# Rotary halves swapped by transfers in place of a permutation product, in a two-layer decoder trunk

## The chip, the cores and the metric

The kernel runs on one core of one Trainium2 chip. Its metric is the device time of one execution in microseconds (us), the median of the timed runs.

## The reference, cut to what matters

Two layers with a residual stream of 1024 positions x 1024 columns in float32. Each layer normalizes, projects, mixes, projects back and runs an MLP. Both layers have queries and keys that are rotated by position before attention:

```python
def apply_rope(x, cos, sin):
    x1, x2 = jnp.split(x, 2, axis=-1)            # two halves of 32 columns of a head of 64
    return jnp.concatenate([x1 * cos - x2 * sin, x2 * cos + x1 * sin], axis=-1)

# layer 0: lightning indexer (iq, ik, iw) picks 256 keys for each query, then attention over them
aq = apply_rope(rms_norm(aq, a_q_norm_g), cos, sin); ak = apply_rope(rms_norm(ak, a_k_norm_g), cos, sin)
iq = apply_rope(iq, cos, sin); ik = apply_rope(ik, cos, sin)
sc = einsum('bqhd,bsd->bqhs', iq, ik)            # index scores, 8 heads
score = einsum('bqhs,bqh->bqs', relu(sc) * 64**-0.5, iw * 8**-0.5)
# layer 1: sliding-window attention with sinks
dq = apply_rope(rms_norm(dq, d_q_norm_g), cos, sin); dk = apply_rope(rms_norm(dk, d_k_norm_g), cos, sin)
```

## The kernel before

The kernel is written with explicit semaphores: each engine has its own list of instructions and works through it in order. Activations lie transposed, 128 features on the partitions. An input projection is cut into units of 128 columns, and each unit into two halves of 512 positions. TensorE computes a half as 24 matmuls (8 blocks of k, three each, of weights and activations split into a high and a low part; lines 2477 to 2479) into one of four PSUM banks in turn. The halves are counted by p. Layer 0 projects, in this order, four units of index queries iq (first all four first halves, then the four second ones), one of index keys ik, four of attention queries aq, one of attention keys ak, and then values and the parts of a recurrence. So p = 0 to 7 is iq, 8 and 9 ik, 10 to 17 aq, 18 and 19 ak. These twenty are the list ROPE0; layer 1 has ten more, ROPE1: two of dk and eight of dq.

What happens to a half that is rotated:

- ScalarE evicts it from PSUM into `xg[:, r % 2, :]` (line 1153 or 1156; r numbers the rotations), for attention queries and keys also its square into `sq` (line 1159), and then raises `proj_free`. Before it overwrites xg it waits for the rotation two before (`rope_done`).
- TensorE, one half later (`follow`), multiplies xg by the constant `rot`, a 128x128 permutation with signs, into PSUM bank 4 (line 2638). The same function adds up the squares (lines 2649 and 2659). `FOLLOWED` lists which halves follow which in the beginning.
- VectorE (`rotate`, line 1831) multiplies bank 4 by sinT into `t2` (line 1838; its rows in the trace name the tile t), xg by cosT (line 1839), and adds the two into its destination (line 1842 or 1849). It raises `rot_read` after the first.

During p = 12 to 19 TensorE also computes the index scores, ten items a half between the blocks of the projection (`scores`, lines 2876 and 2877), in two PSUM banks. ScalarE applies relu into `rl`, which has two buffers (line 1458), and VectorE weights and adds them into `score` (`add_scores`, lines 1876 and 1880). Score product m waits until relu m-2 is done, and relu n waits until sum n-2 is done. In VectorE's list the sums of half p+1 stand ahead of rotation p.

The tables sinT and cosT are made at the start from `positions` and `invf` (lines 1777 to 1791, 1490, 1491). `invf` holds the inverse frequencies, one for each partition.

SyncE's list (SP) holds nearly all loads. Weights come as 512 KB pieces into two raw buffers (`load_unit`, line 649), each when the piece two before has been split into its high part (ScalarE, line 1436) and low part (GpSimd, line 810). Behind them stand, in layer 1, loads of the output weights and of x, and four copies of QS inside SBUF (line 764).

Of the kernel before, what the change touches and what calls it, by code (L numbers as in the profile page):

```python
# [33 lines left out]
HD = 64  # L34
# [42 lines left out]
def build(nc, a, inv_freq, out):  # L77
    with ExitStack() as ctx:
# [6 lines left out]
        def sem(name):  # L85
            return ctx.enter_context(nc.semaphore(name))
# [27 lines left out]
        def const(name, cols, dt=F32, size=4):  # L114
            t = at(name, co[0], [P, cols], dt)
            co[0] += (cols * size + 31) // 32 * 32
            return t

        xn = const("xn", 1024)
        ident, head_ones, rot = const("ident", 128), const("head_ones", 128), const("rot", 128)  # L120
        lmask = at("lmask", co[0], [P, 7, P], I8)
        cbias = const("cbias", 256)
        cT = const("cT", N_ROWS)
# [202 lines left out]
        for n in range(U_ALL):  # L326
# [3 lines left out]
            if not in_halves(n):  # L330
# [2 lines left out]

        raw_landed = [sem(f"raw_landed{i}") for i in range(4)]
        root_begun = sem("root_begun")
        up_first_hi, up_first_lo = sem("up_first_hi"), sem("up_first_lo")
        sums_ready, shared_zero, u_positive = sem("sums_ready"), sem("shared_zero"), sem("u_positive")
        w_hi_ready, w_ready = sem("w_hi_ready"), sem("w_ready")
# [1 line left out]
        own_act, own_dve, own_pool = sem("own_act"), sem("own_dve"), sem("own_pool")  # L340
        (const_landed, cs_saved, cs_landed, consts_built, tables_arg, tables_ready, ct_turned, ct_ready, small_arg,
         small_exp, n_sd, n_xn, n_turned, n_hi, n_lo, proj_done, proj_free, down_done, x_added, u_hi_ready, u_squared, u_ready,
         rot_done, rot_read, rope_done, sq_used, sdq_ready, sdk_ready, rq_ready, iw_turned, iw_ready, ik_copied,
         v_turned, v_ready, sc_done, sc_read, sc_added, thr_ready, level_ready, level_counted, signs_back, gain_landed, vb_saved, lf_ready, b_ready, keys_chosen,
         masks_ready, gw_zero, gw_landed, conv_done, gate_done, gate_read, a_ready, frac_ready, root_ready, oc_ready,
         oc_hi, oc_lo, out_saved) = (sem(n) for n in (
             "const_landed cs_saved cs_landed consts_built tables_arg tables_ready ct_turned ct_ready small_arg "
             "small_exp n_sd n_xn n_turned n_hi n_lo proj_done proj_free down_done x_added u_hi_ready u_squared u_ready "
             "rot_done rot_read rope_done sq_used sdq_ready sdk_ready rq_ready iw_turned iw_ready ik_copied "
             "v_turned v_ready sc_done sc_read sc_added thr_ready level_ready level_counted signs_back gain_landed vb_saved lf_ready b_ready keys_chosen "  # L350
             "masks_ready gw_zero gw_landed conv_done gate_done gate_read a_ready frac_ready root_ready oc_ready "
             "oc_hi oc_lo out_saved").split())
# [286 lines left out]
        def _(sp):  # L639
# [31 lines left out]
            sp.dma_start(posi[:], a["positions"].to_broadcast((P, S))).then_inc(const_landed, 16)  # L671
            sp.dma_start(invf[:], inv_freq).then_inc(const_landed, 16)
            sp.dma_start(sinkb[:], a["d_sinks"].to_broadcast((P, 8))).then_inc(const_landed, 16)
            for n, (_, _, pieces) in enumerate(MIX0):
                if n >= 2:
                    load_unit(n, pieces)
                if n == 3:

                    sp.wait_ge(tables_ready, 2)
                    sp.dma_start(scr_cs[:, 0, :], cosT[:]).then_inc(cs_saved, 16)  # L680
                    sp.dma_start(scr_cs[:, 1, :], sinT[:]).then_inc(cs_saved, 16)
# [55 lines left out]
            load_out(U_OUT0, a["even_w_out"], range(6, N_OUT))  # L737
            load_mlp(U_MLP0, 0)
            for n, (_, _, pieces) in enumerate(MIX1):
                load_unit(U_MIX1 + n, pieces)  # L740
                if n == 2:
                    for t in range(T):
                        sp.wait_ge(x_added, G_MLP0 + S_SUMS * S_ITERS + 2 * t + 2)
                        sp.dma_start(scr_x[:, t, :], x[:, t, :]).then_inc(x_saved, 16)

                    sp.wait_ge(gw_zero, 1)
                    for i, w in enumerate(("c_rgate_w", "c_igate_w")):
                        blocks = a[w][0].rearrange("(n two) c d -> two c n d", two=2)
                        for par in range(2):
                            rows_ = slice(par * HD, par * HD + HD)  # L750
                            sp.dma_start(gw[rows_, 4 * i:4 * i + 4, rows_], blocks[par]).then_inc(gw_landed, 16)
            load_out(U_OUT1, a["odd_w_out"], range(2))
            sp.wait_ge(x_saved, 16 * T)
            sp.wait_ge(oc_ready, 4)
            for t in OC_TILES:
# [29 lines left out]
        def _(pool):  # L785
# [92 lines left out]
                for n in range(n0 + S_UNITS * S_ITERS, n0 + MLP_UNITS):  # L878
                    split_unit(n)

            for t, v in ((ident, 0.0), (head_ones, 0.0), (rot, 0.0), (epsc, EPS), (onec, 1.0)):
                own.link(g.memset(t[:], v))
            own.link(g.affine_select(out=ident[:], in_=ident[:], compare_op=ALU.not_equal, fill=1.0, base=0,
                                     pattern=[[-1, P]], channel_multiplier=1))
            for h in range(2):
                own.link(g.memset(head_ones[h * HD:(h + 1) * HD, h * HD:(h + 1) * HD], 1.0))
            for c, k0, v in ((0, 32, -1.0), (32, 0, 1.0), (64, 96, -1.0), (96, 64, 1.0)):
                own.link(g.affine_select(out=rot[:, c:c + 32], in_=rot[:, c:c + 32], compare_op=ALU.not_equal,
                                         fill=v, base=-k0, pattern=[[-1, 32]], channel_multiplier=1))
            window_and_causal_masks().then_inc(consts_built, 1)  # L890
            def spread_scales(layer, q):

# [820 lines left out]
        def _(dve):  # L1713
# [60 lines left out]

            dve.wait_ge(const_landed, 16 * N_CONST_DMAS)
            link = own.link
            link(v.tensor_copy(pf[:], posi[:]))
            link(v.tensor_scalar(ang[:], pf[:], invf[:, 0:1], None, ALU.mult))

# [51 lines left out]
            def rotate(layer, kind, j, hf):  # L1831
                r = rope_index(layer, kind, j, hf)
                tk = slice(hf * HT, (hf + 1) * HT)
                b = r % 2
                dve.wait_ge(rot_done, r + 1)
                if kind == "ik":
                    dve.wait_ge(iw_turned, hf + 1)
                v.tensor_tensor(t2[:, b, :], ps[:, 4, :], sinT[:, tk], ALU.mult).then_inc(rot_read, 1)
                link(v.tensor_tensor(xg[:, b, :], xg[:, b, :], cosT[:, tk], ALU.mult))
                dve.wait_ge(rot_read, r + 1)  # L1840
                if kind in ("ak", "dk"):
                    link(v.tensor_tensor(t2[:, b, :], xg[:, b, :], t2[:, b, :], ALU.add))
                    dve.wait_ge(sdk_ready, 2 * layer + hf + 1)
                    link(v.reciprocal(key_rms[layer][:], key_rms[layer][:]))
                    dst = (kT if layer == 0 else dkT)[:, tk]
                    v.tensor_tensor(dst, t2[:, b, :], key_rms[layer][:], ALU.mult).then_inc(rope_done, 1)
                else:
                    dst = {"iq": iqT, "aq": qT, "dq": dqT}[kind][:, j, tk] if kind != "ik" else ikT[:, tk]
                    v.tensor_tensor(dst, xg[:, b, :], t2[:, b, :], ALU.add).then_inc(rope_done, 1)
# [44 lines left out]
            for p, (kind, j, hf) in enumerate(ROPE0):  # L1894

                if p == 4:
                    small_arguments()
                if 6 <= p < 9:
                    small_results(p - 6)
                if p == SC_FIRST - 3:  # L1900
                    index_query_low(2)
                    index_query_low(3)
                if p + 2 == SC_FIRST:
                    index_key_low(0)
                if p + 1 == SC_FIRST:
                    dve.wait_ge(iw_ready, 2)
                for n in sc_items(p + 1):
                    add_scores(n)
                rotate(0, kind, j, hf)
                if p + 1 == SC_FIRST:  # L1910
                    index_key_low(1)
            query_scale(0)
# [545 lines left out]
        def _(pe):  # L2458
# [168 lines left out]

            def rope_products(layer, kind, j, hf, p):
                r = rope_index(layer, kind, j, hf)
                pe.wait_ge(proj_free, p + 1)  # L2630
                if r >= 1:
                    pe.wait_ge(rot_read, r)
                if r == 0:

                    pe.wait_ge(n_lo, 14)
                if r == len(ROPE0):
                    pe.wait_ge(gate_read, 8)
                t_.matmul(ps[:, 4, :], rot[:], xg[:, r % 2, :], start=True, stop=True).then_inc(rot_done, 1)
                if kind in ("aq", "dq"):

                    q = sq_index(layer, kind, j, hf)
# [41 lines left out]
            def turn_spread_scales(layer, q):  # L2683
                pe.wait_ge(rq_spread, T * layer + q + 1)
                if layer == 0:
                    bank = (4, 5)[q % 2]
                    if q >= 2:
                        pe.wait_ge(att["q_scaled"], q - 1)
                    elif q:

                        pe.wait_ge(v_ready, 2)
                    else:
                        pe.wait_ge(rot_read, len(ROPE0))
                else:
                    bank = (7, 4)[q % 2]
                    if q >= 2:
                        pe.wait_ge(att["q_scaled"], T + q - 1)
                    else:
                        pe.wait_ge(rot_read, len(ROPE0) + len(ROPE1))
                for j in range(4):  # L2700
                    ins = t_.transpose(ps[:, bank, j * P:(j + 1) * P], rqb[layer][:, q % 2, j * P:(j + 1) * P], ident[:])
                ins.then_inc(att["q_turned"], 1)
# [373 lines left out]
```

## Time and profile before

| | us |
|---|---|
| median of 3 runs | 2543.17 |
| lowest and highest run | 2540.28, 2543.9 |
| span of the profiled execution | 2541.8 |
| TensorE busy in it | 2454.6 |
| VectorE busy | 1611.6 |
| ScalarE busy | 1060.7 |
| GpSimd busy | 1292.5 |

The profile comes from one execution. The execution's own time is not listed apart from its span. Matmuls overlap in it: a row says how long one lasts from its start to its end, and the distance between the starts of two says what one costs TensorE. Bracketed at the end of a row of the order of time is how long the engine had been idle before it, and what ended that. The mean granted clock of TensorE is 0.984 of full speed.

### The profile page before, as it was taken

What the parts mean: (1) busy time and instruction counts of PE and PEld (TensorE: products, weight loads), DVE (VectorE), ACT (ScalarE), POOL (GpSimd) and SP (SyncE); (2) the same over time, 40 slices, a digit from 0 to 9 for tenths busy, and PEclk for the clock granted to TensorE, in tenths of its full rate; (3) what the DMA queues carried; (4) which work ended last, traced back from release to release, by engine and by line L of the source; (5) the groups of instructions that cost most, each with busy time, mean ns of one, the idle gap of its engine ahead of it and who ended that gap; (6) DMA issues with size and microseconds to landing.
All of it is one profiled execution on the core that took longest, in us unless ns stands there. A gap on an engine that the chain in (4) does not pass through costs nothing. (4 is left out here: it accounts for less than half of the span.)

```text
span 2541.8 us, 31069 instructions
## 1 busy us (share of the span) xinstructions
PE 2454.6 (97%) x11111; PEld 1952.5 (77%) x11133; DVE 1611.6 (63%) x2336; ACT 1060.7 (42%) x1821; POOL 1292.5 (51%) x681
## 2 busy tenths in 40 slices
PE   8999998998999999999999999979999999999999
PEld 6778875557888888888888877757687888888887
DVE  6778878988875654465448656675546544564483
ACT  4456887666645332223222356254452322332210
POOL 3212325888863664576449221164337645665490
PEclk9999998999999999999999999979999999999999
DMA  4200121004001210221112231030112111211121
GB/s 150 50 26 26 42 83 51 1 17 133 10 25 51 66 34 33 66 66 50 33 50 59 74 96 42 25 108 13 50 34 67 43 40 50 66 58 33 41 66 67
DMA packets 159545, 133.00 MB, mean 52 GB/s; under 512 B 22537, under 2 KB 134226, under 8 KB 159442
## 3 DMA queue, kind: packets, MB, share of 16 engines
q1 hardware_dynamic: 152978, 125.10, 16.3%
q10 hardware_dynamic: 6464, 6.56, 0.9%
q8 instruction: 61, 1.00, 0.2%
q14 instruction: 42, 0.34, 0.0%
HBM read 116.17 MB, written 13.63 MB: 51 GB/s over the span
## 5 line engine op out<-in xcount | busy, mean ns | idle before, releaser
L2477 PE MATMUL ps<-h_hi,w_hi 128*128 128x512 f32 x1672 | 661.5, 396 | 0.0
L2479 PE MATMUL ps<-h_hi,w_lo 128*128 128x512 f32 x1672 | 651.9, 390 | 0.0
L2478 PE MATMUL ps<-h_lo,w_hi 128*128 128x512 f32 x1672 | 651.4, 390 | 0.0
L810 POOL TENSOR_TENSOR w_lo<-w_raw,w_hi 128x1024 fp32r<-128x1024 f32 x69 | 184.2, 2669 | 361.3 <-ACT w_hi L1436 357.7
L2479 PEld LDWEIGHTS ps<-h_hi,w_lo 128*128 128x128 f32 x1672 | 314.1, 188 | 66.4
L2477 PEld LDWEIGHTS ps<-h_hi,w_hi 128*128 128x128 f32 x1672 | 314.3, 188 | 66.1 <-issue 3.8
L2478 PEld LDWEIGHTS ps<-h_lo,w_hi 128*128 128x128 f32 x1672 | 314.4, 188 | 65.9 <-issue 3.4
L2361 DVE TENSOR_TENSOR x_res<-ps,x_res 128x1024 f32<-128x1024 f32 x224 | 268.7, 1220 | 115.6 <-PE ps L2479 115.6
L828 POOL TENSOR_TENSOR w_lo<-w_raw,w_hi 128x1024 fp32r<-128x1024 f32 x112 | 267.3, 2402 | 127.3 <-ACT w_hi L1298 90.0
L2342 DVE TENSOR_TENSOR u_all<-ps,u_all 128x512 f32<-128x512 f32 x112 | 77.0, 690 | 380.3 <-ACT u_all L1309 380.3
L2477 PE MATMUL ps<-w_hi,uo_hi 128*128 128x512 f32 x784 | 307.9, 393 | 4.9 <-DVE shared L2361 3.5
L2479 PE MATMUL ps<-w_hi,uo_lo 128*128 128x512 f32 x784 | 305.7, 390 | 0.0
L2478 PE MATMUL ps<-w_lo,uo_hi 128*128 128x512 f32 x784 | 305.5, 390 | 0.0
L1309 ACT ACTIVATE u_all<-ps 128x512 f32<-128x512 f32 x112 | 66.7, 599 | 334.0 <-PE ps L2479 333.1
L828 POOL TENSOR_TENSOR w_lo<-w_sum,w_hi 128x1024 fp32r<-128x1024 f32 x42 | 114.0, 2728 | 147.3 <-ACT w_hi L1298 147.3
L2477 PEld LDWEIGHTS ps<-w_hi,uo_hi 128*128 128x128 f32 x784 | 147.1, 188 | 50.5 <-DVE shared L2361 7.7
L1298 ACT ACTIVATE w_hi<-w_raw 128x1024 fp32r<-128x1024 f32 x107 | 111.3, 1052 | 148.8 <-PE ps L2479 148.8
L2479 PEld LDWEIGHTS ps<-w_hi,uo_lo 128*128 128x128 f32 x784 | 147.2, 188 | 31.7
L2478 PEld LDWEIGHTS ps<-w_lo,uo_hi 128*128 128x128 f32 x784 | 147.3, 188 | 27.4
L1301 ACT ACTIVATE uo_hi<-u_all 128x1024 fp32r<-128x1024 f32 x56 | 59.5, 1063 | 161.9 <-PE ps L2479 151.2
L824 POOL TENSOR_TENSOR uo_lo<-u_all,uo_hi 128x1024 fp32r<-128x1024 f32 x42 | 114.9, 2736 | 0.0
L973 POOL TENSOR_TENSOR PL<-PF,h_hi 128x512 fp32r<-128x512 f32 x72 | 104.3, 1460 | 18.1 <-ACT h_hi L1258 17.9
(385 smaller groups left out, 4490.4 us busy)
## 6 DMA issues: line engine op xcount, KB each, us to landing
w_raw<-in_mlp_w_up SPq DMA_DIRECT2D x64, 512.0 KB, 4.1
w_raw<-in_mlp_w_down SPq DMA_DIRECT2D x64, 512.0 KB, 3.6
w_raw<-in_even_w_in SPq DMA_DIRECT2D x23, 512.0 KB, 3.8
x_res<-in_x SPq DMA_DIRECT2D x16, 512.0 KB, 7.9
w_raw<-in_odd_w_in SPq DMA_DIRECT2D x10, 512.0 KB, 3.9
scr_x<-x_res SPq DMA_DIRECT2D x8, 512.0 KB, 2.6
x_res<-scr_x SPq DMA_DIRECT2D x8, 512.0 KB, 4.4
out<-x_res SPq DMA_DIRECT2D x8, 512.0 KB, 2.6
```

Source lines behind the costliest of these rows:

```text
L810: g.tensor_tensor(w_lo[:, k, :], w_raw[:, n % 2, :], w_hi[:, k, :].bitcast(F32), ALU.subtract).then_inc(w_ready, 1)
L824: g.tensor_tensor(uo_lo[o][:], source, uo_hi[o][:].bitcast(F32), ALU.subtract).then_inc(u_ready, 1)
L828: g.tensor_tensor(w_lo[:, slot, :], source, w_hi[:, slot, :].bitcast(F32), ALU.subtract) \
L973: g.tensor_tensor(PL[n % 3][:], PF[n % 3][:], PH[:, n % 3, :].bitcast(F32), ALU.subtract) \
L1298: s.activation(w_hi[:, slot, :], source, ACT.Copy).then_inc(w_hi_ready, 1)
L1301: s.activation(uo_hi[S_OPERAND[k]][:], source, ACT.Copy).then_inc(u_hi_ready, 1)
L1309: s.activation(u_all[:, j, hf * HT:(hf + 1) * HT], ps[:, (h0 + p + UP_BANK) % 4, :], ACT.Relu).then_inc(u_positive, 1)
L2342: v.tensor_tensor(part, src, part, ALU.mult).then_inc(proj_free, 1)
L2361: ins = v.tensor_tensor(dst, ps[:, bank:bank + 2, :], dst, ALU.add)
L2477: t_.matmul(out_, ah, bh, start=first, stop=False)
L2478: t_.matmul(out_, ah, bl, start=False, stop=False)
L2479: return t_.matmul(out_, al, bh, start=False, stop=last)
```

## The change

The product with `rot` goes. In its place SyncE makes four transfers for each rotated half, inside SBUF, of 32 partitions each: rows 32 to 63 of xg go to rows 0 to 31 of t2, 0 to 31 to 32 to 63, and the same for the upper 64. It waits for `proj_free` of that half first, and the four raise `half_moved` of the buffer by 64. The transfers stand at fixed places among the weight loads. VectorE waits for `half_moved`, and its first multiply reads t2 in SBUF instead of bank 4; the signs are put into sinT by negating invf for rows 0 to 31 and 64 to 95. The constant rot and the five instructions that built it go, and so do the waits of TensorE for `rot_read` and those waits for bank 4 that went with it. For attention queries of layer 0 (aq, p = 10 to 17) rotation p now stands ahead of the sums of half p+1 in VectorE's list; for the other kinds the order stays.

```diff
+            def swap_halves(layer, i):
+                r, p = len(ROPE0) * layer + i, i if layer == 0 else H_MIX1 + 16 + i
+                sp.wait_ge(proj_free, p + 1)
+                for to, of in ((0, 32), (32, 0), (64, 96), (96, 64)):
+                    sp.dma_start(t2[to:to + 32, r % 2, :], xg[of:of + 32, r % 2, :]).then_inc(half_moved[r % 2], 16)
+
+            SWAPPED = {3: (0, 1), 4: (2, 3, 4), 5: (5,), 6: (6,), 7: (7,), 8: (8, 9)}
+            SWAPPED.update({n: (2 * n - 8, 2 * n - 7) for n in range(9, 14)})
             for n, (_, _, pieces) in enumerate(MIX0):
                 if n >= 2:
                     load_unit(n, pieces)
+                for i in SWAPPED.get(n, ()):
+                    swap_halves(0, i)
                 if n == 3:
...
             for n, (_, _, pieces) in enumerate(MIX1):
+                if n == 13:
+                    swap_halves(1, 0)
+                    swap_halves(1, 1)
                 load_unit(U_MIX1 + n, pieces)
...
-            load_out(U_OUT1, a["odd_w_out"], range(2))
+            swap_halves(1, 2)
+            swap_halves(1, 3)
+            load_out(U_OUT1, a["odd_w_out"], range(1))
+            for i in range(4, 10):
+                swap_halves(1, i)
+            load_out(U_OUT1, a["odd_w_out"], range(1, 2))
...
-            for t, v in ((ident, 0.0), (head_ones, 0.0), (rot, 0.0), (epsc, EPS), (onec, 1.0)):
+            for t, v in ((ident, 0.0), (head_ones, 0.0), (epsc, EPS), (onec, 1.0)):
...
-            for c, k0, v in ((0, 32, -1.0), (32, 0, 1.0), (64, 96, -1.0), (96, 64, 1.0)):
-                own.link(g.affine_select(out=rot[:, c:c + 32], in_=rot[:, c:c + 32], compare_op=ALU.not_equal,
-                                         fill=v, base=-k0, pattern=[[-1, 32]], channel_multiplier=1))
...
+            for h in range(2):
+                v.tensor_scalar(invf[h * HD:h * HD + 32, :], invf[h * HD:h * HD + 32, :], -1.0, None, ALU.mult)
...
-                dve.wait_ge(rot_done, r + 1)
+                dve.wait_ge(half_moved[b], 64 * (r // 2 + 1))
                 if kind == "ik":
                     dve.wait_ge(iw_turned, hf + 1)
-                v.tensor_tensor(t2[:, b, :], ps[:, 4, :], sinT[:, tk], ALU.mult).then_inc(rot_read, 1)
+                v.tensor_tensor(t2[:, b, :], t2[:, b, :], sinT[:, tk], ALU.mult).then_inc(rot_read, 1)
...
-                for n in sc_items(p + 1):
-                    add_scores(n)
+                if kind != "aq":
+                    for n in sc_items(p + 1):
+                        add_scores(n)
                 rotate(0, kind, j, hf)
+                if kind == "aq":
+                    for n in sc_items(p + 1):
+                        add_scores(n)
...
             def rope_products(layer, kind, j, hf, p):
                 r = rope_index(layer, kind, j, hf)
+                if kind == "iq":
+                    return
                 pe.wait_ge(proj_free, p + 1)
-                if r >= 1:
-                    pe.wait_ge(rot_read, r)
-                if r == 0:
-
-                    pe.wait_ge(n_lo, 14)
                 if r == len(ROPE0):
                     pe.wait_ge(gate_read, 8)
-                t_.matmul(ps[:, 4, :], rot[:], xg[:, r % 2, :], start=True, stop=True).then_inc(rot_done, 1)
```

## Rows read from the trace of the kernel before

**Rows 1.** Windows: start:end, length, busy PE PEld DVE ACT POOL, clock, DMA share, GB/s.

```profile
210.00:240.00 30.00, 30.00 (x139) 24.36 (x138) 26.62 (x70) 15.53 (x25) 8.84 (x6) 1.00 0.13 36
1620.00:1630.00 10.00, 10.00 (x51) 7.87 (x50) 3.18 (x5) 2.35 (x4) 0.00 (x0) 1.00 0.00 1
```

**Rows 2.** Instructions of line 2638, TensorE: duration min/median/max in ns, first and last start.

```profile
L2638 PE MATMUL ps<-xg,rot x60: 590/591/667, 40.7 to 1646.4; 128*128 128x512 f32 x60
```

**Rows 3.** Order of time, TensorE, 52 to 54 us: start, length, instruction, [idle before].

```profile
52.09 0.39 PE L2478 MATMUL ps<-h_lo,w_hi 128*128 128x512 f32 x1
52.32 0.39 PE L2479 MATMUL ps<-h_hi,w_lo 128*128 128x512 f32 x1
...
53.64 0.40 PE L2478 MATMUL ps<-h_lo,w_hi 128*128 128x512 f32 x1
```

**Rows 4.** Order of time, start-up: ScalarE's eviction of half 4, TensorE's products.

```profile
62.05 0.60 ACT L1153 ACTIVATE xg<-ps 128x512 f32<-128x512 f32 x1 [5.75 <-DVE iqT L1849]
...
67.13 1.10 PE L2638 MATMUL ps<-xg,rot 128*128 128x512 f32 x2 [0.88 <-DVE t L1838]
...
76.62 0.39 PE L2478 MATMUL ps<-h_lo,w_hi 128*128 128x512 f32 x1
```

**Rows 5.** Order of time, TensorE, 100 to 191 us: ends of halves, gated score products.

```profile
101.77 1.02 PE L2638 MATMUL ps<-xg,rot 128*128 128x512 f32 x2
...
107.96 0.44 PE L2876 MATMUL ps<-ikH,iqS 128*128 128x384 f32 x1 [0.78 <-ACT rl L1458]
...
177.57 1.02 PE L2638 MATMUL ps<-xg,rot 128*128 128x512 f32 x2
...
184.05 0.47 PE L2876 MATMUL ps<-ikH,iqS 128*128 128x512 f32 x1 [1.07 <-ACT rl L1458]
190.29 1.02 PE L2638 MATMUL ps<-xg,rot 128*128 128x512 f32 x2
```

**Rows 6.** Order of time, one half behind E(16): TensorE, ScalarE, VectorE.

```profile
165.31 1.02 PE L2638 MATMUL ps<-xg,rot 128*128 128x512 f32 x2
167.37 0.59 ACT L1159 ACTIVATE sq<-ps 128x512 f32<-128x512 f32 x1
168.26 0.68 DVE L1838 TENSOR_TENSOR t<-ps,sinT 128x512 f32<-128x512 f32 x1
170.18 5.02 DVE L1880 SCALAR_TENSOR_TENSOR score<-rl,iw,score 128x512 f32<-128x512 f32 x6
171.67 0.50 PE L2876 MATMUL ps<-ikH,iqS 128*128 128x512 f32 x1 [0.57 <-ACT rl L1458]
```

**Rows 7.** DMA issues by line: QS on SP, on ScalarE's queue, a weight load.

```profile
L764 SPq DMA_DIRECT2D QS<-QS x4: 529/604/613, 1663.4 to 1665.3; - x4
...
DMA to landing us min/median/max: 4.0/4.3/5.0
...
DMA to landing us min/median/max: 2.2/2.4/5.1
...
L649 SPq DMA_DIRECT2D w_raw<-in_even_w_in x31: 367/368/1571, 3.1 to 348.8; - x31
```

**Rows 8.** The longest gate and its clock; a shorter gate and its clock.

```profile
135.12 0.33 PE L2876 MATMUL ps<-ikH,iqS 128*128 128x128 f32 x1 [1.74 <-ACT rl L1458]
...
135.95:139.30 3.35, 3.35 (x11) 2.79 (x10) 1.79 (x5) 0.83 (x3) 0.00 (x0) 0.50 0.10 28
...
159.90 0.39 PE L2876 MATMUL ps<-ikH,iqS 128*128 128x256 f32 x1 [1.41 <-ACT rl L1458]
...
160.00:170.00 10.00, 10.00 (x50) 8.23 (x51) 7.44 (x14) 6.51 (x13) 0.00 (x0) 1.00 0.18 50
```

**Rows 9.** VectorE's two multiplies by line: duration min/median/max in ns, first and last start.

```profile
L1838 DVE TENSOR_TENSOR t<-ps,sinT x30: 680/691/694, 49.8 to 1648.9; 128x512 f32<-128x512 f32 x30
L1839 DVE TENSOR_TENSOR xg<-xg,cosT x30: 677/681/2575, 50.4 to 1649.5; 128x512 f32<-128x512 f32 x30
```

**Rows 10.** Order of time, SP's queue, layer 1.

```profile
1611.29 52.09 SPq L774 DMA_DIRECT2D x_res<-scr_x  x2
```

More of the change, by code:

```diff
@@ L119, in build @@
         xn = const("xn", 1024)
-        ident, head_ones, rot = const("ident", 128), const("head_ones", 128), const("rot", 128)
+        ident, head_ones = const("ident", 128), const("head_ones", 128)
         lmask = at("lmask", co[0], [P, 7, P], I8)
@@ L335, in build @@
         root_begun = sem("root_begun")
+        half_moved = [sem("half_moved0"), sem("half_moved1")]
         up_first_hi, up_first_lo = sem("up_first_hi"), sem("up_first_lo")
@@ L342, in build @@
          small_exp, n_sd, n_xn, n_turned, n_hi, n_lo, proj_done, proj_free, down_done, x_added, u_hi_ready, u_squared, u_ready,
-         rot_done, rot_read, rope_done, sq_used, sdq_ready, sdk_ready, rq_ready, iw_turned, iw_ready, ik_copied,
+         rot_read, rope_done, sq_used, sdq_ready, sdk_ready, rq_ready, iw_turned, iw_ready, ik_copied,
          v_turned, v_ready, sc_done, sc_read, sc_added, thr_ready, level_ready, level_counted, signs_back, gain_landed, vb_saved, lf_ready, b_ready, keys_chosen,
@@ L348, in build @@
              "small_exp n_sd n_xn n_turned n_hi n_lo proj_done proj_free down_done x_added u_hi_ready u_squared u_ready "
-             "rot_done rot_read rope_done sq_used sdq_ready sdk_ready rq_ready iw_turned iw_ready ik_copied "
+             "rot_read rope_done sq_used sdq_ready sdk_ready rq_ready iw_turned iw_ready ik_copied "
              "v_turned v_ready sc_done sc_read sc_added thr_ready level_ready level_counted signs_back gain_landed vb_saved lf_ready b_ready keys_chosen "
@@ L2691, in turn_spread_scales @@
                         pe.wait_ge(v_ready, 2)
-                    else:
-                        pe.wait_ge(rot_read, len(ROPE0))
                 else:
@@ L2697, in turn_spread_scales @@
                         pe.wait_ge(att["q_scaled"], T + q - 1)
-                    else:
-                        pe.wait_ge(rot_read, len(ROPE0) + len(ROPE1))
                 for j in range(4):
```

## The prediction

> **What bounds the kernel now.** I read the page's totals first, then TensorE in windows, then its waits, then the order of time around the places that the diff touches. By the totals TensorE is busy for 2454.6 of 2541.8 us, so the first question for each product removed is whether TensorE ran through at that place. In 210 to 240 us and in 1620 to 1630 us it did, with no idle time at full clock [rows 1]. In 100 to 205 us it did not: in seven halves in a row a score product waits for ScalarE's rl, which waits for VectorE (the first at 107.96 us, the last at 184.05 us) [rows 5]. These are the halves in which VectorE adds scores between two rotations, so there the order on VectorE sets the pace, and the diff changes that order.
>
> **The products removed.** The permutation product shows as 60 rows, two passes each, so 30 products (20 in layer 0, 10 in layer 1) [rows 2]. Its cost on TensorE is not its 591 ns a row but the gap that it leaves: one projection matmul starts 0.23 us behind the other; with a product between, 52.32 to 53.64 us is 1.32 us where two steps of 0.23 would do. That is 0.86 us each [rows 3]; 30 would be 25.8 us.
> I part them by place. E(p) is the time at which TensorE ends the projection of half p (the start of the product behind it).
> - Ahead of E(11) = 101.77 us lie ten products, 8.6 us. Twice a second product waited 0.88 us for VectorE to read bank 4, once at 67.13 us [rows 4]; 1.8 us go with it. Sum -10.4 us. The swap must not take TensorE's place as the thing waited for. The nearest cover: half 4 is evicted at 62.05 us after waiting for a rotation, and TensorE needs that bank free only at the half that begins at about 76.6 us [rows 4]; 14 us of cover, less the 6 us by which the work before it gets shorter, against transfers that can lie behind a 512 KB load.
> - Seven products (behind E(11) to E(17)) lie ahead of a wait that VectorE ends. They give nothing by themselves.
> - Three more (behind E(18), E(19) and the next half) lie where no score waits: -2.6 us.
> - Ten in layer 1, with TensorE busy throughout: -8.6 us.
> Gains: 10.4 + 2.6 + 8.6 = 21.6 us. The five GpSimd instructions on rot, and two negations of a 128x1 column in the tables' chain, lie beside the loads of x and are taken at nothing (a few tenths of a us if that cover is gone). The other waits of TensorE on rot_read that go had been met already and give nothing.
>
> **The rotation moved ahead of the sums.** For p = 11 to 17 VectorE now does rotate(p) and then the ten sums of half p+1; before it was rotate(p-1), whose product had been ready for long. VectorE works in order, so while it waits for the swap, the sums of half p+1 queue behind it; rl has two buffers, so relu 2 needs sum 0, and the fifth score product needs relu 2. That is the gate seen now. I take its time from E(p):
> - Before: 107.96 - 101.77 = 6.2 us for p = 11 and 184.05 - 177.57 = 6.5 us for p = 17 [rows 5]; the seven are 6.2, 7.0, 7.5, 6.7, 6.4, 6.4 and 6.5, mean 6.65 us.
> - After: ScalarE ends xg and sq 1.4, 3.2, 2.2, 1.4, 1.6, 2.7 and 1.4 us behind E(p), mean 1.95 (p = 16: 167.37 + 0.59 - 165.31) [rows 6]; then the four transfers, L; then the rotation, 168.26 to 170.18 us = 1.92 us; then from the first sum to the released score product, 170.18 to 171.67 us = 1.49 us [rows 6]. Gate at 5.36 + L.
> L is shown by no row. SP issues them one after another; the nearest kind is the copy of QS inside SBUF, 0.60 us each on SP and 2.2 us from issue to landing at best, 4.3 us where SP's four stood behind a 512 KB load [rows 7]. Three issues ahead of the last and its landing: 3 x 0.62 + 2.2 = 4.1 us, which I take, since no load is issued ahead of these swaps (loads 11, 12 and 13 come behind an odd swap, and wait for nothing else by then). Low end: issues of 0.37 us, as for w_raw [rows 7]: 3.3 us. High end: 1.9 + 4.3 = 6.2 us.
> The gate moves from 6.65 to 9.46 us, so each of the seven halves takes 2.81 us more, 19.7 us in all (14.1 to 34.4 by L's ends). From the gate to E(p+1) TensorE has its own work left, 190.29 - 184.05 = 6.2 us [rows 5], and VectorE's sums (six in 5.02 us, 0.84 each [rows 6]) keep up with it, so nothing is caught up.
> The Trainium skill's page "DMA: Bandwidth & Descriptors", section "Rules for kernel authors", speaks against this order: issue a DMA early, compute, and wait on its semaphore late. The same page, under where a DMA's fixed cost goes, fits about 2.0 us plus bytes over 436 GB/s, an estimate of 2.15 us for 64 KB; the QS copies' 2.2 us [rows 7] agree, and the sum would be the same within 0.4 us.
>
> **The clock.** TensorE, not gated, would reach the fifth score product 4.6 us behind E(p) (107.96 less the idle 0.78, less 101.77, less the product's 0.86 [rows 5]; a little later with wider score products); at 9.5 us it has been idle for some 4.7 us. The longest such idle time now is 1.74 us, at 135.12 us, and behind it the granted clock was 0.50 (1.2 of 2.4 GHz) from about 135.95 to 139.3 us, 3.4 us at half rate, 1.7 us lost [rows 8]. The shorter gates show no such fall: behind the 1.41 us at 159.90 us the clock stays at 1.00 [rows 8]. So I expect a fall at each of the seven; some of the slow time will lie in the idle time, so 1.5 us each, 10.5 us, less the 1.7 us paid already: +8.8 us (bounds -1.7 and +10.2).
>
> **What else queues behind the new waits.** SP now waits for evictions in order. In layer 0 loads 11 to 13 follow an odd swap and are rounded two halves later; load 13 of layer 1 follows the second swap of dk and is used nine halves later. Behind the last swaps of layer 1 stand the load of output unit 1 and that of x tile 4; the loads of x now stop at 1611 us and go on at 1663 us only [rows 10], so a start at about 1640 us has 20 us of cover. Taken at nothing; if the cover of a load were gone, its 4 us.
>
> **The multiply moved to SBUF.** The first multiply read PSUM and stayed within 680 to 694 ns, the second reads two SBUF tiles and went up to 2575 ns beside GpSimd [rows 9]. The change gives the first the second's form. GpSimd splits a weight just behind every other eviction; the rotation now comes some 4 us later, when that has ended. I take nothing, with 0 to 4 us for the range (two of 1.9). The Trainium skill, page "SBUF — State Buffer", on the shared port pair, says that a VectorE instruction with two SBUF inputs and a GpSimd one exclude each other for a whole instruction; the row agrees.
>
> **Sum.** -21.6 + 19.7 + 8.8 = +6.9 us. The profiled span is 2541.8 us, 1.4 us under the median of three runs, 2543.17; I keep that distance, and 2548.7 + 1.4 = 2550.1 us.
>
> **Rivals.**
> - *Faster: the swap is quick and the clock holds.* One mechanism, the length of VectorE's wait in the score halves. With the clock's 8.8 us the change breaks even at L = 3.1 us; if the clock stays full, at 4.6 us. With L = 4.1 us and no fall: -21.6 + 19.7 - 1.7 = -3.6, 2539.6 us. With 3.3 us and no fall: -9.2, 2534.0 us. For it: idle times of up to 1.4 us left the clock alone. Against: 4.7 us is over twice the 1.74 us that did not. With 3.3 us and the falls it is +1.3, 2544.5 us.
> - *A longer landing.* L = 6.2 us, from packets of other transfers or four small transfers that hinder each other: -21.6 + 34.4 + 8.8 = +21.6, 2564.8 us. For it: SP's own row of four is 4.3 us per transfer. Against: a load stood ahead of those.
> - *The change does what it seems made for*: the wait is covered, as if rl were deep enough, and all products and both bank waits go: -25.8 - 1.8 = -27.6, 2515.6 us. Against: the gates now already follow VectorE's position.
> - *The start.* Swaps behind 512 KB loads hold evictions of halves 2 to 9 so long that TensorE waits: two loads of 4 us give +5 on the forecast, 2555 us.
>
> **How the numbers follow.** Chances: forecast 0.40 (its own range 2544 to 2557); clock holds at L = 4.1, 0.17; short L with falls 0.13 and without 0.07; long landing 0.12; all covered 0.04; start 0.07. Slower or faster by 0.2%, about what a measurement of this kernel can tell from no change, is over 2548.3 or under 2538.1 us. Slower: 0.26 of the forecast, long landing, start: 0.45. Faster: the two without falls and short L, all covered, and a third of the clock case: 0.20. Same: 0.35. The range of 8 in 10 reaches from short L without falls to long landing: 2533 to 2565 us.
>
> **What would show it.** Right: VectorE's first multiply in 90 to 200 us waits 3.5 to 5 us for a transfer, seven times; the score product's wait for rl grows from about 1 to 4 us; the clock row falls in most of those halves; E(18) - E(11) grows from 88.5 us to about 117 us; layer 1 from its first rotary half to the attention is 8.6 us shorter. Wrong: VectorE's waits at 2 us or less (L), clock at 1.00 throughout, or TensorE waiting for evictions ahead of E(11).

## The result, and the profile after

| | before | after |
|---|---|---|
| median, us | 2543.5 | 2560.2 |
| lowest and highest run | 2540.28, 2546.41 | 2555.3, 2563.83 |
| ratio of after to before, 95% interval | | 1.0063 [1.0046, 1.0081] |
| span of the profiled execution | 2541.8 | 2553.6 |
| E(11), the projection of half 11 ended | 101.77 | 93.91 |
| E(18) - E(11), the seven score halves | 88.5 | 118.2 |
| last product with gw (layer 1, just ahead of its rotations) | 1578.6 | 1593.8 |
| last product over squares, layer 1 | 1647.6 | 1654.4 |

The change makes the kernel slower, by 0.6%. The span grew by 11.8 us, the median by 16.7 us: the profiled execution is the fastest of the four of after. The same kernel timed again gave 2556.9 us and 1.0060 [1.0047, 1.0073] (below); one of its six executions took 6150.8 us and is not in that interval, which uses undisturbed executions alone.

The totals, from the page of the kernel after:

```profile
span 2553.6 us, 31058 instructions
PE 2440.7 (96%) x11073; PEld 1947.9 (76%) x11073; DVE 1602.6 (63%) x2338; ACT 1059.9 (42%) x1821; POOL 1291.4 (51%) x676
```

TensorE is busy for 13.9 us less than before and the span is 11.8 us longer. So the question is where it waits. As in the prediction, the gate of a half is the score product that has to wait for rl. Line numbers in rows are those of the kernel that was traced, so the same instruction has another number in each version. Waits of the kernel after from 90 to 215 us (us in total, times, longest), and its windows there (columns as in [rows 1]):

```profile
PE ps L2891 <- ACT rl L1475: 29.5, 10, 4.9
DVE t L1857 <- DMA t<-xg: 25.7, 7, 4.9
```

```profile
104.00:110.00 6.00, 5.98 (x29) 5.17 (x29) 4.45 (x9) 3.49 (x7) 0.00 (x0) 1.00 0.00 0
120.40:126.00 5.60, 5.60 (x18) 4.51 (x19) 3.77 (x7) 2.86 (x5) 0.00 (x0) 0.72 0.00 0
138.00:144.00 6.00, 5.89 (x18) 5.03 (x19) 2.62 (x6) 1.53 (x6) 0.00 (x0) 0.50 0.00 0
154.00:160.00 6.00, 5.93 (x19) 4.69 (x20) 4.88 (x8) 3.59 (x8) 0.00 (x0) 0.72 0.00 0
170.60:176.00 5.40, 5.32 (x19) 4.56 (x20) 2.56 (x6) 1.69 (x6) 0.00 (x0) 0.61 0.00 0
188.00:194.00 6.00, 6.00 (x19) 4.89 (x20) 3.47 (x6) 2.55 (x5) 0.00 (x0) 0.68 0.00 0
204.00:210.00 6.00, 5.76 (x18) 4.62 (x19) 3.71 (x7) 2.38 (x5) 0.00 (x0) 0.72 0.01 3
```

The score product's wait for rl was 7.1 us in eight waits before and is 29.5 us now; VectorE's wait for the swap is new. The windows begin at the seven gates: behind six of them the granted clock (the first number behind the brackets) is 0.50 to 0.72, where two score halves of before showed 0.50 and 1.00 [rows 8]. The first, behind an idle time of 2.36 us, stays at 1.00.

The ends of the projections and the gates, TensorE in order of time, kernel after, that answer to [rows 5]:

```profile
93.91 0.95 PE L2668 MATMUL ps<-head_ones,sq 128*128 128x2 f32 x8
...
104.02 0.44 PE L2891 MATMUL ps<-ikH,iqS 128*128 128x384 f32 x1 [2.36 <-ACT rl L1475]
...
109.90 0.95 PE L2668 MATMUL ps<-head_ones,sq 128*128 128x2 f32 x8
...
120.40 0.80 PE L2891 MATMUL ps<-ikH,iqS 128*128 128x512 f32 x1 [4.90 <-ACT rl L1475]
...
195.65 0.95 PE L2668 MATMUL ps<-head_ones,sq 128*128 128x2 f32 x8
...
204.24 0.47 PE L2891 MATMUL ps<-ikH,iqS 128*128 128x512 f32 x1 [4.03 <-ACT rl L1475]
...
212.07 0.95 PE L2668 MATMUL ps<-head_ones,sq 128*128 128x2 f32 x8
```

The product over the squares now stands first behind a projection, so its start is E(p). The gates stand 10.1, 10.5, 9.5, 8.3, 8.8, 10.0 and 8.6 us behind their E(p), mean 9.4 us (6.65 before; 9.46 predicted).

One such half, behind E(16) = 177.97 us, the rows of the relay in order of time (the half of [rows 6], after):

```profile
180.03 0.59 ACT L1176 ACTIVATE sq<-ps 128x512 f32<-128x512 f32 x1
...
180.64 2.41 SPq L680 DMA_DIRECT2D t<-xg  x4
...
184.51 0.69 DVE L1857 TENSOR_TENSOR t<-t,sinT 128x512 f32<-128x512 f32 x1 [3.51 <-DMA t<-xg]
...
186.44 4.17 DVE L1899 SCALAR_TENSOR_TENSOR score<-rl,iw,score 128x512 f32<-128x512 f32 x5
187.28 0.60 ACT L1475 ACTIVATE rl<-ps 128x512 f32<-128x512 f32 x1 [5.60 <-DVE score L1899]
...
187.93 0.79 PE L2891 MATMUL ps<-ikH,iqS 128*128 128x512 f32 x1 [4.90 <-ACT rl L1475]
...
188.53 0.63 PE L2892 MATMUL ps<-ikL,iqS 128*128 128x512 f32 x1
```

Read it as a relay. The square ends at 180.62, four transfers are issued in 2.41 us, and VectorE begins its multiply at 184.51: L = 3.9 us. From there to the gate are 3.42 us (1.92 + 1.49 predicted). Over the seven halves the three parts have these means: evictions end 2.1 us behind E(p) (1.95 predicted), L 4.0 us (4.1), from the multiply to the gate 3.2 us (3.41). In the first of the seven, VectorE did not wait for the swap: it was still at the rotation before. The five sums stand behind the rotation, relu waited 5.60 us for one of them, and the score product waited 4.90 us for relu. The next product lasts 0.63 us in place of 0.39: the clock has fallen.

### The profile page after: what moved, and what is told of

The parts are those of the page before. It is cut to its first block, busy times and chain, and to the rows that moved or that the text cites. A ratio compares the mean times of both kernels' runs of the same rounds, so it can differ in the third digit from the quotient of the medians.

```text
span 2553.6 us, 31058 instructions
## 1 busy us (share of the span) xinstructions
PE 2440.7 (96%) x11073; PEld 1947.9 (76%) x11073; DVE 1602.6 (63%) x2338; ACT 1059.9 (42%) x1821; POOL 1291.4 (51%) x676
## 4 chain that ended last, share of the span: by engine, by line
PE 73%; DVE 10%; ACT 6%; issue 4%; POOL 3%; DMA 1%; SPq 1%; ACTq 0%; DVEq 0%; POOLq 0%
PE ps L2500 21%; PE ps L2502 21%; PE ps L2501 21%; ACT signs L1430 3%; PE ps L2755 1%; POOL cl L1029 1%; PE ps L2493 1%; DMA t<-xg 1%; DVE ub L2387 1%; PE ps L2763 1%; SPq L680 1%; PE ps L2742 1%; PE ps L2783 1%; DVE shared L2384 1%; PE ps L2786 1%
```

## Experiments

The intervals are those of the ratio to the kernel before, timed on the same chip in the same rounds. "After" is the changed kernel.

**The old order with the swaps.**

```diff
-                if kind != "aq":
-                    for n in sc_items(p + 1):
-                        add_scores(n)
+                for n in sc_items(p + 1):
+                    add_scores(n)
                 rotate(0, kind, j, hf)
-                if kind == "aq":
-                    for n in sc_items(p + 1):
-                        add_scores(n)
```

> The changed kernel with VectorE's old order for the attention queries: the sums of half p+1 ahead of rotation p. The swaps by SyncE stay. My theory (VectorE waits for the swap ahead of the sums, and the score products wait for VectorE): no wait of VectorE for a swap is left between 100 and 210 us, the score products' wait falls from 29.6 us to under 7 us, E(18) - E(11) falls from 118.2 us to about 84 us (12.65 us a half less 0.7), the clock stays at full there, and the time is 2513 to 2525 us, some 40 us under the changed kernel and 18 to 30 us under the kernel before. Rival (the transfers themselves cost: SyncE, queues or SBUF): E(18) - E(11) stays over 100 us and the time stays within 5 us of the kernel before or above it.

2529.1 us, 0.9951 [0.9938, 0.9964]: faster than both kernels, by 12 us and by some 28 us. It lies above the expected 2513 to 2525: the 0.7 us a half that was expected from the products taken out did not come. Two of its waits from 90 to 215 us, and its window:

```profile
PE ps L2887 <- ACT rl L1475: 9.9, 11, 2.0
...
DVE t L1857 <- DMA t<-xg: 0.7, 1, 0.7
```

```profile
100.00:210.00 110.00, 100.08 (x465) 80.14 (x464) 91.70 (x134) 61.54 (x114) 11.55 (x6) 0.98 0.19 48
```

With the sums ahead of the rotation the swap has a whole half of time, VectorE waits 0.7 us for it instead of 25.7, and E(18) - E(11) is 182.39 - 93.05 = 89.3 us. That is within 1 us of the 88.5 us of before: the order alone costs the seven halves 29 us, and the seven products taken out of them give nothing there. The span of this profile is 17.8 us shorter than before, by the start (E(11) 8.7 us earlier) and layer 1 (8.4 us); it is the fastest of six executions, and by the medians the gain is 12.5 us.

**Products kept for aq and ak, swaps for the rest.** The version above, with ten of its thirty swaps, those of aq and ak, as products again; iq, ik and layer 1 stay swapped.

```diff
+        def swapped(r):
+            return r < 10 or r >= 20
...
+                if not swapped(r):
+                    t_.matmul(ps[:, 4, :], rot[:], xg[:, r % 2, :], start=True, stop=True).then_inc(rot_done, 1)
```

> Swaps in layer 1 and for iq and ik of layer 0; aq and ak keep their products and the old order of VectorE. Against the variant with all swapped and the sums first (2529 us): if the products behind E(11) to E(17) are worth nothing because VectorE paces those halves, only two products ahead of E(11) and the last three count, up to 4 us, so 2528 to 2534 us. Rival (each product costs 0.86 us there too): 10 us more, 2538 us or above.

2529.9 us, 0.9951 [0.9938, 0.9964]: not to be told from the version with all thirty swaps. E(18) - E(11) is 183.50 - 96.58 = 86.9 us with the products in it, 89.3 us without. So a product in the score halves costs nothing that a run can show. The expectation counted two kept products ahead of E(11); there is none, the first stands at E(11) itself.

The differences that are left are mostly falls of the clock. The third score half has the same work and the same idle time of 1.74 us here and in before: there the clock is at 0.66 from 135 to 140 us and the half takes 14.0 us, here it is at 1.00 from 129.9 to 134.8 us and the half takes 12.5 us. That is the 1.6 us between 88.5 and 86.9. With the swaps, the first and the fifth half are 1.9 and 1.6 us longer than here, with a clock of 0.78 (94 to 99 us) and 0.69 (150.5 to 156 us) in them.

**Swaps in layer 1 alone.** The kernel before, with its ten last products replaced.

```diff
+        def swapped(r):
+            return r >= 20
```

> The kernel before, with the swaps by SyncE in layer 1 alone; layer 0 keeps its products, in the old order. (The signs sit in sinT for both layers, and rot is a permutation without signs.) My theory: ten products of 0.86 us go where TensorE never idles, so the time is 8.6 us under the kernel before, 2532 to 2536 us, and nothing else moves by over 1 us up to the layer. Rival (SyncE's waits and transfers cost something in layer 1): less than 5 us under it.

2534.5 us, 0.9962 [0.9951, 0.9974], so 9 us under before where 8.6 were forecast. From the last product with gw to the last one over squares its trace is 8.4 us shorter than before, as that of after is. TensorE runs through there, and a product costs its whole gap.

**The clock by itself.** After, with sixteen products whose results nobody reads put into the idle time ahead of the gate. VectorE's wait stays; only TensorE is not idle in it.

```diff
+                        if m == items[4] and p < 19:
+                            for _ in range(16):
+                                t_.matmul(ps[:, 4, :], h_hi[:, 0, 0:P], h_hi[:, 0, 0:HT], start=True, stop=True)
```

> The changed kernel with 16 idle-time matmuls (128x512, into the free PSUM bank 4, read by nobody) on TensorE just ahead of the fifth score product of halves 12 to 18, where it stands idle for 3.8 to 4.9 us. They take 3.7 us at full clock. If the clock falls behind each idle time cost what I said (10.5 us in all), it stays at 1.00 from 100 to 210 us and the time falls by 6 to 11 us against the changed kernel, to about 2550 us. If the clock's fall costs nothing (VectorE's sums set the pace in the slow time as well), the time stays within 3 us of the changed kernel's 2560 us although the clock row stays full. If the matmuls do not fit into the idle time, it is slower by up to 5 us.

2547.9 us, 1.0024 [1.0015, 1.0033], against 1.0060 and 1.0063 without: some 0.37%, 9 us faster, for added work. Two of its waits from 90 to 215 us and two windows behind gates:

```profile
DVE t L1857 <- DMA t<-xg: 28.8, 8, 5.8
...
PE ps L2894 <- ACT rl L1475: 7.0, 11, 2.2
```

```profile
120.00:126.00 6.00, 3.77 (x17) 2.81 (x16) 5.54 (x8) 2.40 (x4) 0.00 (x0) 1.00 0.00 0
137.00:143.00 6.00, 5.70 (x30) 4.52 (x29) 5.05 (x9) 2.12 (x6) 0.00 (x0) 1.00 0.22 65
```

VectorE waits no less (28.8 us, 25.7 in after), the clock is at 1.00 where it was 0.72 and 0.50, and E(18) - E(11) is 205.24 - 94.90 = 110.3 us instead of 118.2. The two parts of the loss come apart: 110.3 - 88.5 = 21.8 us are the later gates, 7.9 us the clock. The 7.9 us are the least that the clock takes, since the sixteen products, 3.7 us, are longer than the first half's idle time and hold its gate back by 1.5 us. The rows of after alone part the same 29.7 us into 19.1 us ahead of the gates (seven times 9.38 - 6.65) and 10.5 us behind them.

**Fewer and more transfers.** The swap of after in two transfers of 64 partitions, and in eight of 32 partitions and half a row. The two exchange the heads in place of the halves of a head, so that kernel computes other values with the same bytes moved; the eight move what after moves. The edit of the two:

```diff
-                for to, of in ((0, 32), (32, 0), (64, 96), (96, 64)):
-                    sp.dma_start(t2[to:to + 32, r % 2, :], xg[of:of + 32, r % 2, :]).then_inc(half_moved[r % 2], 16)
+                for to, of in ((0, 64), (64, 0)):
+                    sp.dma_start(t2[to:to + 64, r % 2, :], xg[of:of + 64, r % 2, :]).then_inc(half_moved[r % 2], 16)
```

> The changed kernel with two transfers of 64 partitions for each rotated half in place of four of 32 (same bytes; it swaps the two heads in place of the halves of a head, so the rotation's values are others). L, from the eviction's end to VectorE's first multiply, falls by two issues of 0.6 us, from about 4.0 to 2.8 us. If the wait of VectorE is passed on one to one, the seven gates come 1.2 us earlier each and E(18) - E(11) falls by 8.4 us from 118.2 us, with less idle time for the clock perhaps by up to 5 us more; the time is 2547 to 2552 us. Rival (landing, not issue, makes up L): below 3 us of change.

> The changed kernel with eight transfers of 32 partitions x 256 columns for each rotated half in place of four of 512 columns (same bytes, same result). Four more issues ahead of the last landing: L grows by 2.4 us, the seven gates come 2.4 us later each, E(18) - E(11) grows by about 17 us from 118.2 us, and the time is 2575 to 2582 us; the clock's loss stays the same. The start may lose 1 to 3 us more. Rival (a loss fixed per half, as from the clock alone): within 4 us of the changed kernel.

Two transfers: 2550.8 us, 1.0034 [1.0021, 1.0048]. Eight: 2587.7 us, 1.0181 [1.0166, 1.0196], 6 us over the upper end of what was expected. The mean gate moves from 9.4 us behind E(p) to 8.5 us and to 11.9 us: two issues fewer take off 0.9 us (two of 0.6, less a landing that is 0.3 us longer), four more add 2.6 us. E(18) - E(11) is 113.6 us (8.4 us under 118.2 were expected) and 138.8 us. The issues of the two kernels (KB each, median us from issue to landing), and of the one with eight the waits from 90 to 215 us:

```profile
t<-xg SPq DMA_DIRECT2D x60, 128.0 KB, 2.3
```

```profile
t<-xg SPq DMA_DIRECT2D x240, 32.0 KB, 1.9
```

```profile
DVE t L1859 <- DMA t<-xg: 41.6, 9, 7.3
...
PE ps L2893 <- ACT rl L1477: 32.4, 8, 7.3
...
PE ps L2685 <- ACT xg L1172: 9.4, 1, 9.4
```

A transfer lands in 1.9 us at 32 KB, 2.0 at 64 and 2.3 at 128, so what counts most is how many are issued one behind the other. Eight also hit the start: TensorE waited 9.4 us once for an eviction, and E(11) was 104.1 us, 10 us later than in after. That is the rival on the start, in sight once the swap is slow enough; with the halves' 20.6 us over after it makes up the 30.7 us between this version and the repeat of after.

**After again.** No edit.

> The changed kernel once more, unedited, to place its time on the same chip as the variants and to see how far single executions scatter: 2555 to 2565 us.

2556.9 us, 1.0060 [1.0047, 1.0073]. The ratio repeats within its interval, and so do the seven halves: E(18) - E(11) is 215.50 - 96.16 = 119.3 us. The start does not: E(11) = 96.16 us, 2.3 us later than in after, with two waits of TensorE for evictions (4.0 us; 3.3 in after) and a clock of 0.87 from 80 to 93 us (1.00 in after).

So one trace does not say what the start gives. All versions whose start has the same swaps at the same places show E(11) at 93.05 (old order), 93.91 (after), 94.90 (filler products), 96.16 and 96.58 us (products kept), 5.2 to 8.7 us ahead of before. With products at the start two traces agree: 101.77 us in before and in the version with layer 1 alone.

**Loads ahead of swaps at the start.** The start gave 7.9 us and not 10.4 us, in after and nearly so in the old order. Here each load from unit 5 on stands ahead of the swaps that it stood behind, in the old order of sums (the edit of that order is left out).

```diff
-            SWAPPED = {3: (0, 1), 4: (2, 3, 4), 5: (5,), 6: (6,), 7: (7,), 8: (8, 9)}
-            SWAPPED.update({n: (2 * n - 8, 2 * n - 7) for n in range(9, 14)})
+            SWAPPED = {3: (0, 1), 5: (2, 3, 4), 6: (5,), 7: (6,), 8: (7,)}
+            SWAPPED.update({n: (2 * n - 10, 2 * n - 9) for n in range(9, 15)})
```

> The variant with all swapped and the sums first, with each weight load of layer 0 from unit 5 on put ahead of the swaps that it stood behind. Between 58 and 90 us ScalarE waits 10.3 us for weight loads that SyncE issued only after a swap. If that wait holds the evictions and makes up the 2.5 us that I missed ahead of E(11), then ScalarE's waits for w_raw go, E(11) comes 2 to 3 us earlier and the time is 2525 to 2528 us. Rival (the swaps now land later behind the loads, and hold the evictions as long): 2529 us or more.

2532.5 us, 0.9959 [0.9946, 0.9972]: no gain over the old order's 0.9951 [0.9938, 0.9964], so the rival holds; a loss is not shown. Waits of the kernel from 34 to 100 us:

```profile
ACT xg L1170 <- DVE iqT L1868: 21.9, 7, 8.3
DVE t L1857 <- DMA t<-xg: 8.9, 4, 6.9
...
PE ps L2679 <- ACT xg L1170: 4.8, 1, 4.8
```

ScalarE's wait for w_raw (10.5 us in the old order with swaps first) is gone, and in its place it waits 21.9 us for rotations (11.1 before the edit), since VectorE waited up to 6.9 us for a swap. E(11) is 97.98 us, behind all five traces above.

**The swaps of iq and ik issued by ScalarE.** Both queues of the start apart: loads on SyncE, swaps behind their own evictions on ScalarE. The old order of sums again.

```diff
-            SWAPPED = {3: (0, 1), 4: (2, 3, 4), 5: (5,), 6: (6,), 7: (7,), 8: (8, 9)}
+            SWAPPED = {}
...
                     s.activation(xg[:, r % 2, :], src, ACT.Copy).then_inc(proj_free, 1)
+                    act.wait_ge(proj_free, p + 1)
+                    for to, of in ((0, 32), (32, 0), (64, 96), (96, 64)):
+                        act.dma_start(t2[to:to + 32, r % 2, :], xg[of:of + 32, r % 2, :]).then_inc(half_moved[r % 2], 16)
```

> The kernel with the old order of sums and rotations (sums of half p+1 ahead of rotation p for aq too), and the ten swaps of iq and ik issued by ScalarE right behind its own eviction instead of by SyncE among the loads; the ten others of layer 0 and layer 1's ten stay on SyncE. Theory (the start's shortfall comes from loads and swaps in one in-order queue): ScalarE's waits for w_raw (10.5 us with the swaps on SyncE) nearly go, without the wait of VectorE for a swap growing to 6.9 us as with the loads put first; the half before the first attention-query sums ends near 91.5 us instead of 93.05, so 1 to 2 us under the version with SyncE's swaps: 2526 to 2529 us. Rival (ScalarE's own time is short here: four issues of some 0.6 us for a half on the engine that evicts and splits weights): TensorE waits for evictions, the half ends at 95 us or later, 2531 us or more.

2531.3 us, 0.9963 [0.9951, 0.9975], E(11) = 98.45 us: the rival again, and again no loss beyond the intervals. In order of time, and the waits from 34 to 100 us:

```profile
52.80 2.68 ACTq L1173 DMA_DIRECT2D t<-xg  x4
...
61.04 0.69 DVE L1860 TENSOR_TENSOR t<-t,sinT 128x512 f32<-128x512 f32 x1 [7.03 <-DMA t<-xg]
```

```profile
DVE t L1860 <- DMA t<-xg: 12.0, 5, 7.0
...
PE ps L2682 <- ACT xg L1170: 3.6, 2, 2.1
```

The swap was issued from 52.80 us and its multiply began at 61.04, though no load stood ahead of it in ScalarE's queue. The issues cost ScalarE 2.4 to 3.5 us a swap as well. So the place in the queue is not all of it. The windows of this kernel, then of after:

```profile
50.00:60.00 10.00, 10.00 (x46) 8.29 (x45) 3.88 (x6) 1.22 (x3) 0.00 (x0) 1.00 0.97 254
```

```profile
50.00:60.00 10.00, 10.00 (x46) 8.29 (x45) 5.36 (x10) 1.20 (x2) 0.00 (x0) 1.00 0.71 212
```

The DMA share (the number ahead of the last) is 0.97 here, 0.71 in after. From the end of the eviction to the multiply this swap takes 52.78 to 61.04 = 8.3 us here and 5.8 us in after, against 3.9 us in the score half above (3.9 to 4.6 in the seven), where the share of 10 us is at most 0.32. In the same 10 us the old order had 0.60 and 6.4 us, the loads ahead 0.91 and 8.1 us. The two highest shares go with the two longest swaps. That loads and swaps share the DMA engines fits; which packet waited for which was not measured.

## Why the prediction was right, point by point

- **Sign and size.** 2550.1 us was forecast, with 2533 to 2565 around it; 2560.2 us came out (2556.9 in the repeat), above or at the end of the forecast's own narrower range, 2544 to 2557. The span grew by 11.8 us where the sum had 6.9; the other 4.9 us between the medians lie in the profiled execution being a fast one. Part of the closeness is luck: two stretches that the sum did not have, of -5.5 and +5.0 us, cancel (below). The 0.20 for faster and 0.35 for same are 0.17 and 0.38 by the parts given for them.
- **The gate.** The largest term, and right in its parts: mean gate 9.4 us behind E(p) (9.46), L = 4.0 us (4.1), 3.2 us from the multiply to the gate (3.41). The gates lie 19.1 us later in all (19.7); with the clock held, the halves took 21.8 us more. VectorE waited 3.4 to 4.9 us for a transfer in six halves, not seven.
- **The clock.** 8.8 us forecast, 7.9 us or somewhat more by the version with filler products. The step that judged each gate by the length of its own idle time does not hold: behind 1.74 us of idle the clock fell in before [rows 8] and stayed at 1.00 in the version with products kept, behind 2.00 and 2.04 us in the old order it stayed once and fell to 0.69 once, and 2.36 us left it at 1.00 at 104 us in after. It fell behind all six longer ones, 3.82 to 4.90 us. What decides between the short ones, these runs don't show.
- **Seven products give nothing.** Shown by 89.3 us with the swaps in the old order and 86.9 us with the products, where the 2.4 us between them go for the most part with two falls of the clock. Half by half a little is there: the fourth half, whose gate is only 0.21 us in before, is 0.8 us shorter without its product, and the next half takes it back.
- **Layer 1.** 8.4 us in the trace of after and 9 us by its own version (8.6). SyncE's queue there was right at nothing: no load was late in it. VectorE waited 13.7 us there for swaps, in six waits of up to 4.0 us, and TensorE not once: the same transfers cost nothing where no other work stands behind them.
- **The multiply moved to SBUF.** Right at nothing. All thirty, of the kernel after, by line (min/median/max in ns), with the landing of its transfers:

```profile
L1857 DVE TENSOR_TENSOR t<-t,sinT x30: 677/691/694, 49.5 to 1657.8; 128x512 f32<-128x512 f32 x30
```

```profile
DMA to landing us min/median/max: 1.9/2.0/4.2
```

  None was stretched beside GpSimd as the multiply by cosT had been [rows 9]; the 0 to 4 us kept for it were not needed. The reason given holds as well: GpSimd's split in a score half had ended just before (131.82 + 2.39 = 134.21, multiply at 134.68 us). Where the two meet, the price is there. The version with ScalarE's swaps, in order of time:

```profile
67.48 2.35 POOL L830 TENSOR_TENSOR w_lo<-w_raw,w_hi 128x1024 fp32r<-128x1024 f32 x1 [31.55 <-ACT w_hi L1456]
...
67.70 2.69 DVE L1860 TENSOR_TENSOR t<-t,sinT 128x512 f32<-128x512 f32 x1 [1.83 <-DMA t<-xg]
```

  The same multiply lasts 2.69 us, to 0.6 us behind the end of GpSimd's (0.69 us alone). The Trainium skill's page "SBUF — State Buffer", section "SBUF: two separate sides", says that of a VectorE instruction with two SBUF inputs and a GpSimd one that reads SBUF, the one that starts first holds the shared port pair for its whole length and the other waits. The trace agrees.
- **The start: the term that was mis-sized.** -10.4 us forecast, -7.9 us in the trace of after, -5.2 to -8.7 us over five traces. The prediction named TensorE waiting for evictions ahead of E(11) as a sign of being wrong, and this sign came. "14 us of cover" was counted for one eviction; what was left out is that SyncE issues a load only when the swaps ahead of it have had their evictions, and that ScalarE, which splits the loads, evicts too. SyncE, VectorE, ScalarE and TensorE of after, in order of time:

```profile
52.26 10.90 SPq L680 DMA_DIRECT2D t<-xg  x12
...
58.01 0.69 DVE L1857 TENSOR_TENSOR t<-t,sinT 128x512 f32<-128x512 f32 x1 [4.54 <-DMA t<-xg]
...
60.13 0.60 ACT L1170 ACTIVATE xg<-ps 128x512 f32<-128x512 f32 x1 [5.96 <-DVE iqT L1868]
...
63.20 1.24 SPq L650 DMA_DIRECT2D w_raw<-in_even_w_in  x2
...
67.96 1.06 ACT L1453 ACTIVATE w_hi<-w_raw 128x1024 fp32r<-128x1024 f32 x1 [5.30 <-DMA w_raw<-in_even_w_in]
...
78.25 1.06 ACT L1453 ACTIVATE w_hi<-w_raw 128x1024 fp32r<-128x1024 f32 x1 [4.48 <-DMA w_raw<-in_even_w_in]
...
79.85 0.65 PE L2683 MATMUL ps<-ident,xg 128*128 128x128 f32 x4 [1.36 <-ACT xg L1170]
```

  The loads at 63.20 us stood behind twelve issues of swaps, ScalarE waited 5.30 us for one of them, and TensorE waited for evictions, 3.3 us in two waits ahead of E(11). In the other four traces the clock was at 0.87 or 0.88 from 80 to 93 us, which the prediction had not counted for the start either. That the loads behind swaps are the cause is argued from these rows, not shown: with the loads ahead, ScalarE's wait for them was gone and E(11) no earlier. No arrangement that gives the whole 10.4 us was found.
- **Three more products.** -2.6 us forecast; from E(18) to E(20) the delay against before falls from 21.8 to 20.6 us, so 1.2 us of the two products there shows. The third lies behind E(20), in the stretch of the next point.
- **Not forecast.** The delay shrinks from 20.6 us at E(20) to 15.1 us when the products with gw begin (1505.4, 1520.6 us), and from the last rotation to the end it grows by 5.0 us again. The sum had 0.9 us of this, the third product. Much of the rest can be the scatter of single executions: the version with layer 1 alone runs the work of before up to there and begins the same products 3.1 us earlier (1502.3 us), and behind the last rotation it is 1.1 us longer than before. No run was made to part these.
- **The rule on DMAs.** The Trainium skill's page "DMA: Bandwidth & Descriptors", section "Rules for kernel authors", says: "Issue the DMA early, do compute, wait on its semaphore late". It spoke against this change, and the version that follows it is 1.1% under after. The fit of the same page that the prediction took for a landing is given there for transfers that GpSimd issues; its 2.15 us stand beside 2.0 us measured here for SyncE's.

## What to carry to other kernels

Replacing an instruction of the busiest engine by transfers pays where that engine runs through (9 us for ten here) and gives nothing where it waits for another engine anyway; look at the waits of each stage first. Place the wait for a transfer in a list behind work that does not need it: here that order alone decides between -0.5% and +0.6%. An idle time of TensorE can cost twice, by itself and by the clock behind it: 21.8 and 7.9 us here.

## What the runs showed of the hardware

- Swaps of 32 partitions inside SBUF land 1.9 us after the issue at 32 KB each, 2.0 at 64 KB, and 2.3 at 128 KB with 64 partitions; SyncE needs some 0.6 us for each issue (four in 2.41 us), ScalarE the same or more (2.44 to 3.50 us for four).
- Products without use in an idle time of TensorE made a kernel 9 us faster; the granted clock stayed at 1.00 (2.4 GHz) in the windows shown, where it had been 0.72 and 0.50 (0.50 is 1.2 GHz).
- The length of one idle time does not tell whether the clock falls behind it: behind 1.74 us the windows showed 0.66 in one trace and 1.00 in another with the same work, and behind 2.36 us 1.00. All six of 3.82 to 4.90 us in after were followed by 0.50 to 0.72.
- A swap of the same four transfers of 64 KB took from 3.9 us (DMA share up to 0.32) to 8.3 us (0.97) from the end of the eviction to the multiply.
- A VectorE multiply of two SBUF tiles went from 0.69 to 2.69 us when it began 0.22 us behind a GpSimd multiply of 2.35 us, and stayed at 0.69 us beside none.
